# Two transformer blocks on one core: exponents of the linear attention by halves of 64 tokens, and the second block's heads in pairs

## The reference, cut to what matters

```python
bcum = jnp.cumsum(ac, axis=2)
o_inter = jnp.einsum('bhtd,bhde->bhte', qc * jnp.exp(bcum), s)
decay = jnp.exp(jnp.where(mask[:, :, None], diff, -jnp.inf))
att = jnp.einsum('bhtd,bhsd,bhtsd->bhts', qc, kc, decay)
```

## Time and profile before

| what | value |
|---|---|
| median of 3 runs | 4097.31 us (4089.55 to 4106.05) |
| the profiled execution | 4107.89 us, span 4105.8 us |
| TensorE busy | 3850.4 us, 94% |
| DVE, ACT, GpSimd busy | 1879.8, 993.8, 1965.1 us |
| linear attention, layers 0 and 1 | 629.0 and 478.7 us |
| heads stage of the second block, its first four query tiles included | 506.0 us |

### The profile page before, as it was taken

One profiled execution on the slowest core, in us unless ns is written; L12 is line 12 of the kernel. 1 busy time (PEld: TensorE's weight loads), 2 busy tenths in 40 slices (PEclk: granted clock), 3 DMA queues, 4 the chain that ended last, 5 costly groups with the idle time before them and its releaser, 6 DMA issues. The chain is left out here.

```text
span 4105.8 us, 51266 instructions
## 1 busy us (share of the span) xinstructions
PE 3850.4 (94%) x19583; PEld 3048.2 (74%) x19583; DVE 1879.8 (46%) x2689; ACT 993.8 (24%) x1744; POOL 1965.1 (48%) x834
## 2 busy tenths in 40 slices
PE   7999999999988998899999999899799999999999
PEld 4777788888877887676678888777585555577877
DVE  3444335645548883344426656466214444463200
ACT  3333112222210001333312222100214544412200
POOL 2433342332335554344453443688443333387886
PEclk9999999999999999999999999999899999999999
DMA  6211221211226543222232221344422222253333
GB/s 211 49 44 48 77 48 42 53 40 42 53 66 123 118 99 111 67 57 58 60 79 58 54 62 49 92 92 129 128 53 72 65 55 66 63 159 77 97 88 92
DMA packets 485311, 317.84 MB, mean 77 GB/s; under 512 B 38185, under 2 KB 456370, under 8 KB 483210
## 3 DMA queue, kind: packets, MB, share of 16 engines
q1 hardware_dynamic: 466080, 288.59, 28.6%
q10 hardware_dynamic: 19050, 26.75, 1.9%
HBM read 282.71 MB, written 32.56 MB: 77 GB/s over the span
## 5 line engine op out<-in xcount | busy, mean ns | idle before, releaser
L938 POOL TENSOR_TENSOR whi<-ring,con 128x1024 fp32r<-128x1024 f32 (+1 forms) x415 | 978.7, 2358 | 2085.7 <-DMA ring<-in_w_in 1597.8
L615 PE MATMUL ps<-xT_parts,whi 128*128 128x512 f32 (+2 forms) x2632 | 1019.1, 387 | 71.0 <-DVE zz L2225 18.3
L615 PE MATMUL ps<-hT_parts,whi 128*128 128x512 f32 (+1 forms) x2864 | 1050.4, 367 | 0.0
L940 POOL TENSOR_TENSOR ring_parts<-ring,whi 128x1024 fp32r<-128x1024 f32 (+1 forms) x415 | 989.4, 2384 | 32.5
L615 PE MATMUL ps<-xT_parts,ring_parts 128*128 128x512 f32 (+2 forms) x2600 | 946.8, 364 | 0.0
L615 PE MATMUL ps<-arena_parts,whi 128*128 128x512 f32 (+1 forms) x2344 | 726.0, 377 | 53.7 <-DVE arena_parts L2257 36.1
L1651 ACT ACTIVATE arena<-ps 128x768 f32<-128x768 f32 (+9 forms) x561 | 298.6, 542 | 1638.4 <-PE ps L615 786.2
L615 PE MATMUL ps<-arena 128*128 128x128 f32 (+9 forms) x3292 | 642.2, 338 | 11.9 <-DVE arena L2225 9.0
L615 PEld LDWEIGHTS ps<-xT_parts,whi 128*128 128x128 f32 (+1 forms) x2632 | 501.6, 191 | 177.5 <-issue 87.8
L615 PEld LDWEIGHTS ps<-hT_parts,whi 128*128 128x128 f32 x2864 | 544.9, 190 | 89.9 <-issue 7.2
L615 PEld LDWEIGHTS ps<-arena 128*128 128x128 f32 (+3 forms) x3292 | 433.9, 192 | 166.9 <-issue 130.3
(11 more groups left out here) (173 smaller groups left out, 3644.2 us busy)
## 6 DMA issues: line engine op xcount, KB each, us to landing
ring<-in_w_in SPq DMA_DIRECT2D x504, 256.0 KB, 4.1
arena<-in_w_ada SPq DMA_DIRECT2D x64, 256.0 KB, 5.9
ring<-in_w_up SPq DMA_DIRECT2D x64, 256.0 KB, 4.0
ring<-in_w_down SPq DMA_DIRECT2D x64, 256.0 KB, 3.9
ring<-in_w_out SPq DMA_DIRECT2D x48, 256.0 KB, 3.9
gates_kept<-stage ACTq DMA_DIRECT2D x24, 384.0 KB, 4.1
arena<-gates_kept SPq DMA_DIRECT2D x24, 384.0 KB, 3.8
arena<-in_w_ada SPq DMA_DIRECT2D x8, 1024.0 KB, 19.7
```

What stands on the lines that cost most here:

```text
L615: return nc.tensor.matmul(o, l, r, start=first, stop=last)
L938: v.tensor_tensor(hi, raw, ones[:, 0:m].unsqueeze(1).to_broadcast([P, kt, m]), ALU.mult).then_inc(w_rounded, 1)
L940: v.tensor_tensor(ringR[:, s, 0:kt, 0:m], raw, hi.bitcast(F32), ALU.subtract).then_inc(w_split, 1)
```

## The change

**Exponents by halves.** A sum over a level's stretch never crosses the middle of the 128 tokens. The constant matrix keeps, for the seven levels, only the own half of each token: 7x64 = 448 columns for rows 0 to 63 and 448 for rows 64 to 127; the two sums over the whole unit (256 columns) stay on 128 rows. A full unit now takes four matmuls of 64 rows x 448 columns, in turn on the upper and the lower half of the rows and into banks 2 and 3, and two of 128 rows x 256 columns into bank 4. ACT takes Exp in two instructions (896 and 256 columns) with a wait on itself between them. DVE makes four products (896, 896, 128, 128 columns) in place of two of 1024, with one more level in their access patterns.

**Heads in pairs.** The units are reordered so that c0 and c1, or g = 0 and g = 1 of the same queries, are neighbours (cmp stays four of g = 0, then four of g = 1), and scores are issued for two units at once, at even n for n+2 and n+3, after the waits of both. Values of the two groups are interleaved matmul by matmul; they write rows 0 to 63 and 64 to 127 of one bank. The transposed probabilities lie in four triangular buffers. DVE does normalise(n) ahead of maximum(n+2). The first gate tile is multiplied ahead of all scores; the plan of the fill is made anew from changed costs.

```diff
-        gE = bank(2, 9 * P).rearrange("p (c m) -> p c m", c=9)
+        gE_half = [bank(2 + c, LEVEL_COLS) for c in range(2)]
+        gE_levels = bank(2, 1024).rearrange("p (c n) -> p c n", c=2)[:, :, 0:LEVEL_COLS]
+        gE_sums = bank(4, 2 * P).rearrange("p (c m) -> p c m", c=2)
...
-                        pieces = [(2 + c, c * 512, w) for c, w in ((0, 512), (1, 512), (2, P))] if full else \
-                            [(2, 0, P), (4, 8 * P, P)]
-                        for c, at, w in pieces:
+                        if full:
                             for h in range(2):
-                                last = mm(bank(c, w), gla_parts[h][:, d, t], sums_part[:, d, at:at + w], h == 0, h == 1)
+                                for c, rows in enumerate((slice(0, 64), slice(64, P))):
+                                    mm(gE_half[c], gla_parts[h][rows, d, t], sums_part[rows, d, 0:LEVEL_COLS], h == 0, h == 1)
+                        for h in range(2):
+                            last = mm(bank(4, 2 * P), gla_parts[h][:, d, t], sums_part[:, d, LEVEL_COLS:SUM_COLS], h == 0, h == 1)
...
-                        e = gE if units[j][2] else gE[:, 0:9:8]
-                        do(e, e, ACT.Exp).then_inc(e_ready, 1)
+                        if units[j][2]:
+                            own(do(gE_levels, gE_levels, ACT.Exp))
+                            own.settle()
+                        do(gE_sums, gE_sums, ACT.Exp).then_inc(e_ready, 1)
...
-                            own(v.tensor_tensor(gqE[:, j % 3].rearrange("p (l t) -> p l t", l=8), gE[:, 0:8], q_, ALU.mult))
-                            ins = v.tensor_tensor(gkE[:, j % 2].rearrange("p (l t) -> p l t", l=8), gE[:, 1:9], k_, ALU.mult)
-                        else:
-                            ins = v.tensor_tensor(gkE[:, j % 2, 7 * P:8 * P], gE[:, 8], gk[:, t * P:(t + 1) * P], ALU.mult)
+                            for dst, x in ((gqE[:, j % 3], gq), (gkE[:, j % 2], gk)):
+                                x = x[:, tokens].rearrange("p (c t) -> p c t", c=2).unsqueeze(2).to_broadcast([P, 2, LEVELS, 64])
+                                own(v.tensor_tensor(dst[:, 0:2 * LEVEL_COLS].rearrange("p (l c t) -> p c l t", l=LEVELS, c=2),
+                                                    gE_levels.rearrange("p c (l t) -> p c l t", l=LEVELS), x, ALU.mult))
+                            own(v.tensor_tensor(gqE[:, j % 3, 7 * P:8 * P], gE_sums[:, 0], gq[:, tokens], ALU.mult))
+                        ins = v.tensor_tensor(gkE[:, j % 2, 7 * P:8 * P], gE_sums[:, 1], gk[:, tokens], ALU.mult)
...
-            for kind, g, subs in (("A", 0, ("c",)), ("B", 0, ("b",)), ("B", 1, ("b",)),
-                                  ("C", 0, ("sel", "win", "cmp")), ("C", 1, ("sel", "win", "cmp"))):
+            for kind, sub, groups in (("A", "c", (0,)), ("B", "b", (0, 1)), ("C", "sel", (0, 1)), ("C", "win", (0, 1)),
+                                      ("C", "cmp", (0,)), ("C", "cmp", (1,))):
...
-        VALUES_AT = [("A", 0, 8, 2), ("B", 0, 17, 2), ("B", 1, 19, 2), ("C", 0, 28, 3), ("C", 1, 40, 3)]
+        VALUES_AT = [("A", 8, 2), ("B", 17, 2), ("sel", 25, 2), ("win", 33, 2), ("cmp0", 36, 1), ("cmp1", 41, 1)]
...
-            if n + 3 < 4 * NS2:
-                total += 2 * (heads2[n + 3]["w"] / 1200 + 0.1)
+            if n % 2 == 0 and n + 2 < 4 * NS2:
+                total += 3 * (heads2[n + 2]["w"] / 1200 + 0.1)
...
+            def scores(n):
+
+                for b, q, k in [operands(n + c) for c in range(2)]:
+                    mm(b, q, k, True, True).then_inc(scores2, 1)
...
+                elif kind in ("sel", "win"):
+                    for s in range(LT):
+                        for g in range(2):
+                            todo.append((bank(1)[rows[g], s * P:], (vS if kind == "sel" else vW)[:, s, rows[g]],
+                                         pT_keys(use[g], s, s * P, LAT - s * P), kind == "sel" and s == 0, False))
...
+            pe.wait_ge(w_split, splits.number() + 1)
+            for k in range(KT):
+                fill_step(k)
             pe.wait_ge(n2_ready, NORM0 + 4)
-            for n in range(3):
-                scores(n)
+            scores(0)
             for n in range(4 * NS2 + 3):
                 i, m = divmod(n, NS2)
-                if n + 3 < 4 * NS2:
-                    scores(n + 3)
+                if n % 2 == 0 and n + 2 < 4 * NS2:
+                    scores(n + 2)
...
+            product()
+            do(gate_out2[0], bank(2).rearrange("p (a n) -> p a n", a=2), ACT.Tanh, scale=0.5).then_inc(gate2_tanh, 1)
+            tiles.next()
             exp(0)
             exp(1)
...
             for n in range(4 * NS2):
                 i, m = divmod(n, NS2)
+                normalise(n)
                 if n + 2 < 4 * NS2:
                     maximum(n + 2)
-                normalise(n)
```

More of the change, by code:

```diff
@@ L523, in two_blocks @@
         for i in range(4):
-            pT_use = 7 * i
-            for kind, g, subs in (("A", 0, ("c",)), ("B", 0, ("b",)), ("B", 1, ("b",)),
-                                  ("C", 0, ("sel", "win", "cmp")), ("C", 1, ("sel", "win", "cmp"))):
[L527 to L530, removed]
+            for kind, sub, groups in (("A", "c", (0,)), ("B", "b", (0, 1)), ("C", "sel", (0, 1)), ("C", "win", (0, 1)),
+                                      ("C", "cmp", (0,)), ("C", "cmp", (1,))):
+                for qt in range(LT):
+                    lo = max(qt - 1, 0) * P if kind == "B" else 0
+                    w = NB2 if sub == "cmp" else (qt + 1) * P - lo
+                    for g in groups:
+                        use = None if sub == "cmp" else 7 * i + {"c": 0, "b": 1, "sel": 3, "win": 5}[sub] + g
@@ L563, in unit_us @@
             total = 0.0
-            if n + 3 < 4 * NS2:
-                total += 2 * (heads2[n + 3]["w"] / 1200 + 0.1)
+            if n % 2 == 0 and n + 2 < 4 * NS2:
+                total += 3 * (heads2[n + 2]["w"] / 1200 + 0.1)
             if n < 4 * NS2 and heads2[n]["sub"] != "c0":
                 total += 0.1 + 0.11 * -(-heads2[n]["w"] // P)
-            for kind, g, first, per in VALUES_AT:
+            for kind, first, steps in VALUES_AT:
                 j, o = divmod(n - first, NS2)
-                if 0 <= j < 4 and o < (2 if kind != "C" else 3):
-                    total += {"A": 1.1, "B": 0.9, "C": 1.3 if o == 2 else 2.2}[kind]
+                if 0 <= j < 4 and o < steps:
+                    total += {"A": 1.1, "B": 1.0, "sel": 1.3, "win": 1.3}.get(kind, 0.9)
             return total
@@ L608, in turned_round, with pT_at, pT_keys, pT_block @@
             return bass.AP(x.tensor, x.offset + P - 1, dims[:-1] + [[-1, P]])
-        def pT_slot(use):
-            return use % 3 * LT
+        def pT_at(use, s, q):
+            at, step = (0, LAT) if use % 2 == 0 else (LT * LAT, -(LAT + P))
+            return KT * ALL + use % 4 // 2 * 5 * LAT + at + step * s + q
+        def pT_keys(use, s, q, n):
+            o = pT_at(use, s, q)
+            return arena[:, o:o + n]
+        def pT_block(use, s, blocks, q):
+            first = pT_keys(use, s, q, P)
+            return bass.AP(first.tensor, first.offset + P - 1,
+                           [list(first.ap[0]), [pT_at(use, 1, 0) - pT_at(use, 0, 0), blocks], [-1, P]])
         def mm(o, l, r, first, last):
@@ L1533, in turn, with values @@
                 last.then_inc(turned2, 1)
[L1535 to L1539, removed]
+            def values(i, kind, step, steps):
+                mine = [u for u in heads2 if u["i"] == i and
+                        (u["kind"] == kind or u["sub"] == kind or u["sub"] + str(u["g"]) == kind)]
+                use = {u["g"]: u["use"] for u in mine}
+                rows = [slice(g * 64, g * 64 + 64) for g in range(2)]
@@ L1560, in values @@
-                for args in sum(steps[step * per:(step + 1) * per], []):
+                        for s in range(max(t - 1, 0), t + 1):
+                            for g in range(2):
+                                todo.append((bank(1)[rows[g], t * P:(t + 1) * P], vB[:, s, rows[g]],
+                                             pT_keys(use[g], s, t * P, P), s == max(t - 1, 0), s == t))
+                elif kind in ("sel", "win"):
+                    for s in range(LT):
+                        for g in range(2):
+                            todo.append((bank(1)[rows[g], s * P:], (vS if kind == "sel" else vW)[:, s, rows[g]],
+                                         pT_keys(use[g], s, s * P, LAT - s * P), kind == "sel" and s == 0, False))
+                else:
+                    g = int(kind[-1])
+                    todo.append((bank(1)[rows[g], :], vc[0:NB2, g], pTcmp[0:NB2], False, True))
@@ L1561, in values @@
+                per = -(-len(todo) // steps)
+                for args in todo[step * per:(step + 1) * per]:
                     last = mm(*args)
-                if (step + 1) * per >= len(steps):
+                if step + 1 == steps:
```

82 lines of the change are left out of this document (40 added, 42 removed).

## The result

The changed kernel took 4119.4 us (median of 14 runs, 4112.8 to 4132.4) and the kernel before, run beside it, 4101.5 us (14 runs, 4089.6 to 4106.3): ratio 1.0053, 95% interval 1.0044 to 1.0061. So it is slower, by about the half per cent that a measurement here can tell. The forecast was 4099 us with a range of 4045 to 4140; the range holds the time, and the single number is 20 us low.

The account below looks back on a forecast made before the run. TensorE was taken to bound both attention layers and the heads. Heads +7 us (-77 + 73 + 11) and attention -5 gave +2 on the profiled 4107.9; with the median 10.6 below that execution, 4099 us, range 4045 to 4140.

Parts of the forecast that it names:

- exponents: Linear attention: a full unit's exponents take 0.97 us instead of 1.10, over 80 units -11 us.
- fresh waits of the attention: Waits on keys(0) in layer 1 and behind z tiles in layer 0: chain about 0.5 us longer, +6 us.
- heads, work saved (scores, switches, values): Heads: overlapped score columns -32 us, fewer form switches -19, values halved -23.
- heads, waits, first gate tile included: Heads: exposed waits behind fresh scores +92 us, old waits gone -19, first gate tile covering a wait -3.
- heads, clock: Heads: 14 falls of the clock to half, 8 more than before, +11 us.
- heads in all: Heads: -77 us saved, +73 of waits and +11 of clock, sum +7 us.
- rival 3: Attention: the fp32r halves don't overlap, +29 us, 4128 us in all; chance 0.08.
- rival 2: Heads: all 33 exposed places drop the clock, 19 more falls of 1.7 us, 4131 us in all; chance 0.17.
- Rival 1: Heads: exposed waits are half of the walk, -46 us and -7 for the clock, 4046 us in all; chance 0.30.
- the deciding point: Heads: the slower-by-the-clock case decides the outcome from about 26 falls in the stage.
- Rival 4: Heads: no pair overlaps, kept apart by waits or increments between matmuls, +54 us, 4153 us in all; chance 0.03.

Follow-up runs that it names:

- e2: The kernel before with all the edits of the heads and none of the attention's: 4126.9 us, ratio 1.0043 to the kernel before.
- e9: The changed kernel with its pairs of scores issued earlier, at odd n for n+3 and n+4: 4039.4 us, ratio 0.9848 to the kernel before.
- e10: The changed kernel with score pairs issued at odd n for n+3 and n+4, and ACT's tanh, square and copy ahead of exp(n+2): 4014.8 us, ratio 0.9796.
- e7: The kernel before with only ACT's order changed, tanh, square and copy ahead of exp(n+2): 4087.2 us, ratio 0.9972.
- e3: The changed kernel with only ACT's order changed, tanh, square and copy ahead of exp(n+2): 4057.8 us, ratio 0.9876 to the kernel before.

## Why the prediction was right, and where it was off

Each step of the sum, as it was put, and what the runs showed:

| term | forecast | shown |
|---|---|---|
| exponents | -11 | -13 |
| fresh waits of the attention | +6 | +6 |
| clock in the attention | not in the sum | +3 in layer 0, -1 to -2 in layer 1 |
| heads, work saved (scores, switches, values) | -74 | -70 to -74 |
| heads, waits, first gate tile included | +70 | +74.5 |
| heads, clock | +11 | +19 to 22 |
| heads in all | +7 | +22.7 |

The rows of the heads are counted up to the output product, where both kernels have done the same work.

**The overlap** was right, fp32r too: the sum's assumption holds and rival 3 is out. The price of the form switch was right as a whole: in layer 1 the matmul ahead of the exponents takes 0.33 us to the next start instead of 0.24, the group 0.94 instead of 1.10, and the matmul behind 0.11 instead of 0.16 (medians of the 32 full units, from start to start). That is -0.12 us for each of 80 units, where -0.13 was forecast. What was wrong is how it divides. The two of a pair start 3 to 6 ns apart for fp32r and 6 to 7 ns for fp32, where I allowed 0.07 us. The Trainium skill (TensorE: Matmul & The Clock Gate, Part 3) has about 4 ns between tiles, and the trace agrees in size. The switch around the exponents costs about 0.35 us instead of 0.28 + 0.05: an estimate, 0.94 + 0.09 - 0.05 of the group and its neighbours less 0.63 for two times 448 and two times 256 columns at the pace of full-array matmuls. In the heads the scores fell by 51 us of busy time (111.1 to 59.9), where 32 + 19 was forecast, and the values by 22.5 (57.8 to 35.3), where 23 was.

**A term left out:** the 16 units of layer 1 that only carry the state also went from four matmuls to two (line 1336 of before, "pieces" without the levels). They save 0.20 us each by the same reading, 3 us. Nor was the clock of layer 0 priced: it was at half for 41.2 us instead of 34.1. Over the nine executions with the exponents by halves layer 0 takes 627.5 to 631.2 us, with the old ones 627.2 to 633.8 (three): no gain, since the 5 us of work that it is spared are taken up by 3 us more of idle time and about 3 us for the clock. Layer 1 is 470.3 to 473.0 against 478.7 to 478.8, a gain of 6. The attention as a whole gave 6 where 5 was forecast, in one layer instead of both.

**The waits of the heads** were the boldest step, a walk through the plan's arithmetic, and it held: 74.5 us more idle time where 70 was forecast. A gate tile's wait without other cover was put at 2 us, 3.3 with the table load, less a turn; the trace has 22 places, up to 3.2. The shape was wrong: I said 33 places of 2 us or more, and there are 46 of more than 1 us and 11 of 2 us or more. The kernel before has 7 of more than 1 us. That the sum comes so close is in part luck: the walk took places too long and too few.

**The clock** is the term that was mis-sized. I took 14 falls from 33 long places; 17 begin in the stretch, and several stand behind waits of only 1.3 to 1.8 us. The starting point was off as well: I counted six falls in the heads before, and seven begin there, two of them twice as long as the rest. What I held against rival 2, that waits of about 1 us often left the clock alone, that trace hardly shows: each of its 7 waits of more than 1 us lies in a fall or has one within 3 us; only one of 1.00 us (3312.24) has none. The time at half rose by 41 us up to the drain (37.2 to 78.2) and by 45 up to the output product (37.2 to 82.5), where 8 falls of 3.4 us had been added. Four pairs of executions price it, in us of busy time for each us at half: e2 against the changed kernel 0.43, e9 against e10 0.46, before against e7 0.48, the changed kernel against e3 0.41 (the last three differ in order too). I had 0.5, so the price was a little high and the time at half much too short. It makes 19 to 22 us instead of 11, and with the waits, 4.5 us over the forecast, the heads come to +22.7 instead of +7.

**Rival 1**, waits half as large, is out: the idle time is there in full. What the prediction held against it, that the order of ACT's queue leaves no way past exp(n+2), was the right reason; e3, which opens that way, brings the idle time to 52 us and the stage to 469, near the 460 that this rival gives it (506 + 7 - 53). Rival 2 named the clock as what turns the sum, and half of the miss is that, with fewer falls: it put the deciding point at 26, and with 17, several of them long, and 4.5 us more of waits the half per cent was reached. Rival 4 is out by the groups by form. The prediction called itself wrong if the heads came to over 530 us. Up to the drain, as it cut them, they came to 532; up to the output product they grew by 22.7 us, which on 506 is 529. So by its own bound, as it was cut, its account of the heads fails, if only just, and the clock's term is what carries it there. The total is in the range without luck, since the range reaches 41 us over the forecast: the heads' +22.7 and the attention's -5.7 make 17 us, and the medians differ by 17.9 (4101.5 to 4119.4). The profiled executions differ by less, 8.3 us of span, because the rest of that execution was 8.7 us shorter, which no part of the change explains.

## What to carry to other kernels

When two units are issued together, count the iterations between the issue and the first reader's place in its queue, for the earlier unit of the pair; a pair issued in the same iteration as its reader can turn every step behind that reader into a wait. Price such waits twice, as idle time and as the clock that falls behind them: here 75 us of waits brought some 20 us more. Two changes that look like one gain (an earlier issue, a better order in a queue) are compared on one chip, and by the stage rather than by the whole.

## What the hardware showed

- Matmuls on separate halves of rows or columns start 3 to 7 ns apart and run at full speed beside each other, fp32 and fp32r alike: two scores of 512 columns take 1.06 us to the next start, one alone takes 1.05. The Trainium skill (TensorEngine Tiling (Array Packing), Key Properties) says that changing the mode drains the engine; the price here is 0.09 us on the matmul ahead (0.33 us to the next start instead of 0.24) and about 0.2 us in the scores (1.05 us where the columns take 0.85), 0.3 in all for going in and out again.
- The granted clock doesn't answer to single waits. With the lead and the order (e10) there are 11 waits of 1.1 to 1.9 us in the heads and no fall begins there; in the changed kernel, with 46 waits of more than 1 us, it fell behind some of 1.3 us (a wait of 1.29 us ends at 3342.22, the fall begins at 3342.49). What the clock did around the wait of 2.63 us above, in four stretches of the changed kernel (columns as in the earlier trace rows):

```profile
3114.10:3117.50 3.40, 3.01 (x14) 1.93 (x12) 2.71 (x9) 1.62 (x5) 3.32 (x2) 1.00 0.01 2
3117.50:3120.90 3.40, 1.18 (x5) 0.30 (x4) 2.11 (x8) 1.40 (x4) 0.14 (x1) 0.96 0.68 145
3120.90:3124.30 3.40, 2.99 (x7) 1.52 (x9) 0.87 (x4) 3.15 (x6) 2.25 (x1) 0.50 0.06 10
3124.30:3127.70 3.40, 3.40 (x12) 2.55 (x11) 2.84 (x6) 1.49 (x5) 2.47 (x2) 0.54 0.02 5
```

  TensorE is busy for 1.18 us of the second stretch; the clock then stands at half (1.2 GHz) through the third and nearly all of the fourth, 7 us in all, although the engine is busy again in both. Five of the seven falls that begin in the heads before lasted half as long, as the one of the earlier trace rows. What decides between the two was not tried.
- ACT's load of a function table takes 1.28 us and is placed ahead of the wait of the instruction that needs it, so it is free when that wait is long (before) and stands in the chain when the instruction is late (3199.77 above).
